# Hybrid attention and MoE layer: expert rows summed in four PSUM banks over the whole pass, picks that carry the row scale, more of expert 13 kept, half loads in the last turn

## The chip, the core and the metric

The kernel runs on one core of a Trainium2 chip. A core has TensorE (PE, matrix products into PSUM), VectorE (DVE), ScalarE (ACT), GpSimd (POOL) and SyncE (SP, which here only issues transfers), an on-chip memory SBUF of 128 partitions, and the accumulator memory PSUM with 8 banks of 128 x 512 floats. Transfers from HBM are issued on queues and carried by 16 DMA engines. The metric is the device time of one execution in microseconds; lower is better. The span of a profiled execution goes from its first to its last instruction.

## What is computed

One layer over 256 tokens plus 16 meta tokens, width 1024, in float32. First a mixer (two attentions side by side, gates, an output projection that is added to the residual), then a mixture of experts, and a final norm:

```python
h = h + mix[:, :T]
hn = rms_norm(h, norm_ffn_g[l])
# moe_ffn(hn): top 4 of 32 experts for each token, softmax over the four
gu = xb @ w_gate_up[e] + b_gate_up[e]                 # 1024 -> 2048
x_glu = minimum(x_glu, 7.0); x_lin = clip(x_lin, -7.0, 7.0)
act = x_glu * sigmoid(1.702 * x_glu) * (x_lin + 1)
yb = act @ w_down[e] + b_down[e]                      # 1024 -> 1024
out[token] += yb * gate
h = h + out
return rms_norm(h, norm_final_g)[:, N_META:]
```

Every expert is read whole: 8 MiB of gate-up weights and 4 MiB of down weights, 32 times, 403 MB in all.

## The kernel before, in words

**Stages.** Up to about 240 us the mixer runs; its weights come in through a ring of small slots. Then the residual `h1` (two tiles of 128 tokens) is normed, the router picks experts, and one pass over the 32 experts follows, until about 1152 us. Each expert has up to `CAP` = 64 rows in a pass; with more, a further pass would run (`n_pass`, read from memory at run time; here it is 1). Then come the final norm and four stores.

**Slots and loads.** The expert weights go through four slots of 4 MiB (`eslot(0)` to `eslot(3)`, two in the tensor `arena`, two in `ring`). A pass has 96 loads of one slot each, in the order gate-up first half, gate-up second half of an expert, and its down rows behind those of the next expert. SP waits until a slot is free (`slot_free`, on `wide_used`, which TensorE raises), then issues the load of four places later. The first eight refills are cut into quarters (`first_refill`), then come whole loads (`whole_load`), and `last_loads` cuts the last five into halves, the very last into a half and two quarters. TensorE waits for loads in `arrived`. `KEPT` = 3 of the eight gate-up chunks of expert 29 (3 MiB) are loaded ahead, during the mixer's end, into memory that is free by then, and left out of the load of that expert.

**The order on TensorE.** It is written out by hand. Ahead of the loop: projection, router products, counting of ranks in bank 7, and `gather_first`, which collects the rows of experts 0 and 1. A gather is a product of the row-scaled residual `hs` (made by ScalarE, in two copies) with a 0/1 matrix `pick` made by VectorE. Then `gate_up` of expert 0, a transposition of the biases and `features` (eight transpositions of rows into features). The loop goes over turns of two pairs of experts; `expert_pair` does, for experts x and x+1: `gate_up` of x+1, `pick_rows`, `down` of x, `gather` for the next pair, `scatter` of x, `gate_up` of x+2, `features`, `pick_rows`, `down` of x+1, `features`, `scatter`. `last_pair` is its end form. `scatter` multiplies the expert's rows with the gated pick and leaves the 256 x 1024 result in banks 4 to 7, and VectorE adds those banks to `h1` each time (`add_rows`, two additions of 128x1024 for an expert). TensorE waits for the first of them (`s_acc`) before it uses banks 4 to 7 again. After `BIAS_TURN` = 3 turns the gated down biases are multiplied once and added in the same way.

**The other engines.** VectorE also makes the picks, adds biases, clamps and forms the activation; ScalarE copies PSUM rows to SBUF and does the sigmoid. At the end VectorE multiplies `h1` by the final gain, which a transfer has put on all 128 partitions (`gfin`).

## Time and profile before

| what | us |
|---|---|
| median of 3 runs | 1165.92 (1164.47 to 4083.46) |
| the profiled execution, time | 1165.41 |
| its span | 1163.6 |
| TensorE busy | 1101.5 (95%) |
| VectorE, ScalarE busy | 332.2 (29%), 203.7 (18%) |
| read from HBM | 432.13 MB |

How to read it: TensorE's share is high, but its rows can overlap and waits between them are short, so the share alone doesn't say that it is the bound. The transfer rate in each slice of the span is the second thing to look at. A row of a timeline gives its start in us from the start of the span, its duration, the engine, the line of the program, the operation and how many instructions stand in it; in brackets is how long the engine was idle before it and what ended that. A matrix product of the source is two such instructions where its operands are full float32.

### The profile page before, as it was taken

The numbers are of one execution on the slowest core, as the hardware profiler recorded it, in microseconds if no ns is written. First come the engines' busy times: TensorE is split into PE (matmuls) and PEld (weight loads), VectorE is DVE, ScalarE is ACT, GpSimd is POOL, SyncE is SP. The second block draws the span as 40 slices with busy tenths as digits, with TensorE's granted clock in tenths as the row PEclk, the third lists the DMA queues.
The fourth block names the chain that finished last, engine by engine and source line by source line (L and its number), as shares of the span: only waits on it lengthen the run. The fifth ranks groups of instructions, "written<-read, shape, count | busy, mean of one in ns | idle before, by whom it ended". The sixth has DMA issues, their size and how long they took to land. (4 is left out here: it accounts for less than half of the span.)

```text
span 1163.6 us, 13610 instructions
## 1 busy us (share of the span) xinstructions
PE 1101.5 (95%) x5490; PEld 526.2 (45%) x5490; DVE 332.2 (29%) x774; ACT 203.7 (18%) x359; POOL 14.2 (1%) x27
## 2 busy tenths in 40 slices
PE   8999999999999989898989998989999999899997
PEld 6878888554343434343434343433333333343433
DVE  2256443132323131313131313131313131313223
ACT  2438781031101010101010101010101010101012
POOL 3010000000000000000000000000000000000000
PEclk9999999999999999999989999999999999999999
DMA  9814237869999999999999999999999999999994
GB/s 309 278 36 128 90 110 291 359 223 423 422 433 431 431 433 430 431 433 430 433 431 432 431 432 430 433 431 431 433 430 433 430 431 433 431 431 431 426 426 164
DMA packets 39750, 433.66 MB, mean 373 GB/s; under 512 B 3160, under 2 KB 19698, under 8 KB 23204
## 3 DMA queue, kind: packets, MB, share of 16 engines
q1 hardware_dynamic: 38160, 429.45, 88.1%
q0 software_dynamic: 960, 2.30, 0.6%
q10 hardware_dynamic: 596, 1.45, 0.4%
q8 instruction: 23, 0.38, 0.1%
q14 instruction: 11, 0.09, 0.0%
HBM read 432.13 MB, written 1.05 MB: 372 GB/s over the span
## 5 line engine op out<-in xcount | busy, mean ns | idle before, releaser
L1738 PE MATMUL psum<-arena 128*64 128x512 f32 x1016 | 224.4, 595 | 11.0 <-DMA arena<-in_w_gate_up 10.9
L1738 PE MATMUL psum<-ring,arena 128*64 128x512 f32 x968 | 217.4, 604 | 9.2 <-DMA ring<-in_w_gate_up 9.2
L1738 PEld LDWEIGHTS psum<-arena 128*64 128x64 f32 x1016 | 70.9, 137 | 156.8 <-issue 139.9
L1754 PE MATMUL psum<-ring,arena 128*64 128x512 f32 x544 | 123.7, 608 | 15.5 <-DMA ring<-in_w_down 9.1
L1738 PEld LDWEIGHTS psum<-ring,arena 128*64 128x64 f32 x968 | 68.2, 139 | 151.1 <-issue 148.8
L1196 DVE TENSOR_TENSOR arena<-psum,biasT 128x512 f32<-128x512 f32 x64 | 44.3, 692 | 292.3 <-PE psum L1710 288.0
L859 DVE TENSOR_TENSOR arena<-psum,vT 128x512 f32<-128x512 f32 (+1 forms) x42 | 28.4, 681 | 341.7 <-PE psum L1637 331.8
L1754 PE MATMUL psum<-arena 128*64 128x512 f32 x480 | 108.0, 603 | 10.4 <-DMA arena<-in_w_down 10.4
L773 ACT ACTIVATE arena<-psum 128x1024 f32<-128x1024 f32 x32 | 32.7, 1023 | 325.1 <-PE psum L1738 311.7
L1754 PEld LDWEIGHTS psum<-ring,arena 128*64 128x64 f32 x544 | 42.2, 140 | 85.5 <-issue 85.5
L1220 DVE TENSOR_TENSOR h<-h,psum 128x1024 f32<-128x1024 f32 x64 | 75.3, 1218 | 16.0 <-PE psum L1779 14.0
L1754 PEld LDWEIGHTS psum<-arena 128*64 128x64 f32 x480 | 35.0, 139 | 73.3 <-issue 67.6
L780 ACT ACTIVATE arena<-arena 128x512 f32<-128x512 f32 x32 | 20.2, 630 | 266.1 <-DVE arena L1204 266.1
L1779 PE MATMUL psum<-kst,wr 64*128 64x512 f32 x256 | 63.6, 615 | 1.6 <-ACT kst L790 1.6
L1637 PEld LDWEIGHTS psum<-arena 128*128 128x128 f32 x512 | 58.4, 192 | 12.9 <-issue 12.9
L1637 PE MATMUL psum<-arena 128*128 128x128 f32 x512 | 61.4, 279 | 0.0
L1587 PE MATMUL psum<-arena,ring 128*128 128x256 f32 x256 | 60.5, 380 | 0.0
L790 ACT ACTIVATE kst<-psum 128x512 f32<-128x512 f32 x32 | 19.1, 597 | 225.7 <-PE psum L1754 225.7
L1587 PEld LDWEIGHTS psum<-arena,ring 128*128 128x128 f32 x256 | 46.3, 190 | 5.6
L1710 PEld LDWEIGHTS psum<-kst,arena 128*128 128x128 f32 x256 | 27.4, 141 | 25.4 <-issue 24.3
L1710 PE MATMUL psum<-kst,arena 128*128 128x128 f32 x256 | 35.0, 280 | 0.8 <-ACT arena L773 0.8
L1779 PEld LDWEIGHTS psum<-kst,wr 64*128 64x128 f32 x256 | 22.2, 186 | 22.5 <-issue 20.7
(233 smaller groups left out, 762.2 us busy)
## 6 DMA issues: line engine op xcount, KB each, us to landing
arena<-in_w_gate_up SPq DMA_DIRECT2D x28, 4096.0 KB, 30.2
ring<-in_w_gate_up SPq DMA_DIRECT2D x27, 4096.0 KB, 30.0
arena<-in_w_down SPq DMA_DIRECT2D x14, 4096.0 KB, 30.1
ring<-in_w_down SPq DMA_DIRECT2D x12, 4096.0 KB, 30.1
ring<-in_w_in SPq DMA_DIRECT2D x14, 1024.0 KB, 12.5
arena<-in_w_gate_up SPq DMA_DIRECT2D x13, 1024.0 KB, 15.9
arena<-in_w_gate_up SPq DMA_DIRECT2D x5, 2048.0 KB, 25.2
ring<-in_w_down SPq DMA_DIRECT2D x10, 1024.0 KB, 16.4
```

The costliest lines, as they stand in the source:

```text
L773: sc.activation(gl.rearrange("q (b j p) -> q b j p", p=P, j=DN_ROWS), banks(home, home + 2).rearrange("q (b p j) -> q b j p", p=P, j=DN_ROWS),
L780: sc.activation(sg, glu, ACT.Sigmoid, scale=1.702).then_inc(s_sig, 1)
L790: sc.activation(yr, bank[1], ACT.Copy).then_inc(s_y, 1)
L859: return v.tensor_tensor(dst, src, vec.unsqueeze(2).broadcast_to([P] + cols), ALU.mult)
L1196: return v.tensor_tensor(dst.rearrange("p (m j) -> p m j", m=8), src, bias[:, m:m + 8, cols(e, 1)].broadcast_to([P, 8, CAP]), ALU.add)
L1220: v.tensor_tensor(half, half, banks(4 + 2 * t, 6 + 2 * t), ALU.add).then_inc(s_acc[t], 1)
L1587: ins = mm(job_bank(name)[:, 0:SEQ], win(8 + m // 2)[:, c, (m % 2) * P:(m % 2 + 1) * P], xnT[:, c, META:KEYS], start=c == 0, stop=c == CH - 1)
L1637: ins = mm(bank[k][:, c * P:(c + 1) * P], hs[:, t, (4 * k + c) * P:(4 * k + c + 1) * P], pick[:, t, :], start=t == 0, stop=t == 1)
L1710: ins = tr(bank[home + m // 4][:, (m % 4) * P:(m % 4 + 1) * P], gl[:, m * P:(m + 1) * P], ident)
L1738: ins = mm(bank[home + n][h * CAP:(h + 1) * CAP, :], xg[:, c, e * CAP:(e + 1) * CAP], w[:, h * D + n * 512:h * D + (n + 1) * 512], start=c ...
L1754: ins = mm(bank[1][n * CAP:(n + 1) * CAP, :], act[:, c * CAP:(c + 1) * CAP], w[:, n * 512:(n + 1) * 512], start=first, stop=last)
L1779: ins = mm(bank[4 + 2 * t + n], pickgT[n * CAP:(n + 1) * CAP, t * P:(t + 1) * P], yr[n * CAP:(n + 1) * CAP, :], start=True, stop=True)
```

## The change

- **Sums in PSUM.** Banks 4 to 7 hold the sum over all experts. Four products with a zero operand (`open_sum`) open them ahead of the loop, every `scatter` accumulates (`start=False`), the down biases accumulate too, and VectorE adds the banks to `h1` once, after the last expert, into `fin`. `add_rows` and its waits are gone. Behind the last gathers of a pass TensorE puts `fin - h1` back into the four banks for a further pass.
- **Other banks.** What used banks 4 to 7 moves: ranks to bank 3, the first `gate_up` and `features` to banks 2 and 3, the odd expert's `features` to banks 0 and 1, `pick_rows` to bank 0. New waits follow: `s_low` for the first expert, `s_pgt` before a gather, `s_lin` before the second `pick_rows`.
- **Picks carry the scale.** `hs` and ScalarE's two copies are gone. The pick matrices are multiplied by the row's scale, the gates are divided by it, and a gather reads `h1` itself, each fourth float (`strided`).
- **Kept rows.** The kept part is now of expert 13 (3 MiB of gate-up) and, new, three of its eight down chunks (1.5 MiB). The two loads that are shortened lie in turn 3, which is written out beside the loop.
- **The end.** The last ten loads, all of the last turn, are halves. The final gain is loaded to one partition and spread by two products in `last_pair`. `BIAS_TURN` is 4.

```diff
-KEPT_EXPERT = EXPERTS - 3
+KEPT_TURN = 3
+KEPT_EXPERT = 2 * UNROLL * KEPT_TURN + 1
+HALVES = TURN_LOADS - GU_LOADS
+KEPT_DN = 3
+KEPT_DN_LOAD = KEPT_LOAD + EXPERT_LOADS + 1
-BIAS_TURN = 3
+BIAS_TURN = KEPT_TURN + 1
...
-                    if idx == KEPT_LOAD:
-                        part_of(idx, rows, 0, QUARTERS - KEPT, whole)
-                    elif left > ESLOT:
+                    if left >= HALVES:
                         part_of(idx, rows, 0, QUARTERS, whole)
                     else:
                         part_of(idx, rows, 0, 2, half_loaded[left])
...
+                loops_of_loads(b, base, 0, kept_at)
+                for idx in range(REFILL_END + kept_at * TURN_LOADS, REFILL_END + (kept_at + 1) * TURN_LOADS):
+                    if idx not in (KEPT_LOAD, KEPT_DN_LOAD):
+                        whole_load(idx, base, 1)
+                        continue
+                    slot_free(idx, base)
+                    part = slice(0, EWIDTH - (KEPT * 2 * D if idx == KEPT_LOAD else KEPT_DN * D))
+                    sp.dma_start(eslot(idx)[:, part], rows_of(idx - GU_LOADS, 1)[:, part]).then_inc(
+                        wide_loaded[idx % ESLOT], 16)
+                loops_of_loads(b, base, kept_at + 1, LOAD_TURNS)
...
+            kept_down = down_rows(KEPT_EXPERT)
+            sp.dma_start(kept_dn[0], kept_down[:, EWIDTH - 3 * D:EWIDTH - 2 * D]).then_inc(s_kdn, 16)
+            sp.dma_start(arena[:, 0:2 * D], kept_down[:, EWIDTH - 2 * D:EWIDTH]).then_inc(s_kdn, 16)
...
-                sc.activation(hs[:, t, :].rearrange("q (b j p) -> q b j p", p=P, j=GU_ROWS),
-                              h1[:, t * D:(t + 1) * D].rearrange("q (b p j) -> q b j p", p=P, j=GU_ROWS),
-                              ACT.Copy, scale=st[:, 22 + t:23 + t]).then_inc(s_hs, 1)
...
+            def first_pick(t):
+                for e in range(2):
+                    ins = v.tensor_scalar(pick[:, t, e * CAP:(e + 1) * CAP], iota, rk3[:, t, e:e + 1],
+                                          st[:, 22 + t:23 + t], ALU.is_equal, ALU.mult)
+                return ins
...
+                for t in range(2):
+                    ins = v.tensor_scalar(pick[:, t, :], pick[:, t, :], st[:, 22 + t:23 + t], None, ALU.mult)
...
-            def add_rows(x):
-                for t in range(2):
-                    dve.wait_ge(s_sc, x * 2 + (t + 1))
-                    half = h1[:, t * D:(t + 1) * D]
-                    v.tensor_tensor(half, half, banks(4 + 2 * t, 6 + 2 * t), ALU.add).then_inc(s_acc[t], 1)
...
-                clamped(mlink, x, 0, 4)
+                clamped(mlink, x, 0, 2, s_low, dve.snap(b * PAIRS + 1))
...
+                v.tensor_copy(gains, banks(2, 4)).then_inc(s_gs, 1)
+                for t in range(2):
+                    dve.wait_ge(s_sc[t], x + EXPERTS)
+                    v.tensor_tensor(fin[:, t, :], h1[:, t * D:(t + 1) * D], banks(4 + 2 * t, 6 + 2 * t),
+                                    ALU.add).then_inc(s_acc[t], 1)
...
-                        ins = mm(bank[k][:, c * P:(c + 1) * P], hs[:, t, (4 * k + c) * P:(4 * k + c + 1) * P],
-                                 pick[:, t, :], start=t == 0, stop=t == 1)
+                        ins = mm(bank[k][:, c * P:(c + 1) * P],
+                                 strided(h1[:, t * D:(t + 1) * D], 4 * k + c, GU_ROWS), pick[:, t, :],
+                                 start=t == 0, stop=t == 1)
...
+            def open_sum(n):
+                mm(bank[n], fmask[:, 0:P], kst[:, 0:512], start=True, stop=False)
...
-                                 yr[n * CAP:(n + 1) * CAP, :], start=True, stop=True)
-                    ins.then_inc(s_sc, 1)
+                                 yr[n * CAP:(n + 1) * CAP, :], start=False, stop=last)
+                    ins.then_inc(s_sc[t], 1)
...
-                for t in range(2):
-                    pe.wait_ge(s_acc[t], x + 1)
+                pe.wait_ge(s_lin, g + 1)
                 pick_rows(x + 1, 1)
-                down(tb, o + 5, x + 1, half_loaded[ESLOT] if ending else None)
+                down(tb, o + 5, x + 1, ending, part_kept)
...
+                for n in range(2):
+                    ins = mm(bank[2 + n], ones[96:97, :], gfin[:, n * 512:(n + 1) * 512], start=True, stop=True)
+                ins.then_inc(s_gb, 1)
                 scatter(x)
...
+                pe.wait_ge(s_minus, 1)
+                for t in range(2):
+                    pe.wait_ge(s_acc[t], b + 1)
+                    for n in range(2):
+                        col = slice(n * 512, (n + 1) * 512)
+                        mm(bank[4 + 2 * t + n], ident, fin[:, t, col], start=True, stop=False)
+                        ins = mm(bank[4 + 2 * t + n], minus, h1[:, t * D + n * 512:t * D + (n + 1) * 512], start=False,
+                                 stop=False)
+                ins.then_inc(s_again, 1)
```

Three places show how instructions move. First TensorE, ahead of the loop over the passes, from the rank count of the second tile's first half to the first `gate_up`. Before (1645 is `gather_first`, 1628 the router, 1695 and 1696 the rank count):

```order
L1645 MATMUL psum<-arena 128x128 x4
L1628 MATMUL psum<-wr,arena 128x32 x4
L1645 MATMUL psum<-arena 128x128 x4
L1695 MATMUL psum<-rk,kst 128x32
L1696 MATMUL psum<-rk,kst 128x32
L1645 MATMUL psum<-arena 128x128 x4
L1701 TENSOR_LOAD npi
L1701 ISA x2
L1645 MATMUL psum<-arena 128x128 x4
```

And now (1675 is `gather_first`, 1657 the router, 1728 `open_sum`, 1733 and 1734 the rank count):

```order
L1675 MATMUL psum<-arena,h 128x128 x4
L1657 MATMUL psum<-wr,arena 128x32 x4
L1675 MATMUL psum<-arena,h 128x128 x4
L1728 MATMUL psum<-kst 128x512
L1733 MATMUL psum<-rk,kst 128x32
L1734 MATMUL psum<-rk,kst 128x32
L1728 MATMUL psum<-kst 128x512 x2
L1675 MATMUL psum<-arena,h 128x128 x4
L1728 MATMUL psum<-kst 128x512
L1742 TENSOR_LOAD npi
L1742 ISA x2
L1675 MATMUL psum<-arena,h 128x128 x4
```

Four openings stand between the rank count and the last gather, and the gathers read `h`. Second, SP's queue between the mixer's last weights and the first refills, now (590 and 597 are expert 0's and 1's gate-up loads, 592 and 599 kept gate-up rows, 594 and 595 are new):

```order
L590 DMA arena<-in_w_gate_up 128x8192 x2
L592 DMA arena<-in_w_gate_up 128x2048
L594 DMA arena<-in_w_down 128x1024
L595 DMA arena<-in_w_down 128x2048
L597 DMA ring<-in_w_gate_up 128x8192
L599 DMA arena<-in_w_gate_up 128x4096
L585 DMA ring<-in_w_gate_up 128x4096
```

The two new loads stand behind the first kept one and ahead of a wait. Third, the end of TensorE's program. Before (1754 is `down`, 1779 `scatter`, 1748 `pick_rows`, 1637 `gather`):

```order
L1754 MATMUL psum<-ring,arena 64x512 x16
L1779 MATMUL psum<-kst,wr 128x512 x4
L1748 MATMUL psum<-kst,arena 128x128 x2
L1754 MATMUL psum<-ring,arena 64x512 x16
L1779 MATMUL psum<-kst,wr 128x512 x4
L1637 MATMUL psum<-arena 128x128 x16
```

And now (1802, 1832, 1796 and 1666 in their places; 1906 spreads the gain, 1927 and 1928 put the sums back):

```order
L1802 MATMUL psum<-ring,arena 64x512 x16
L1906 MATMUL psum<-arena,kst 128x512 x2
L1832 MATMUL psum<-kst,wr 128x512 x4
L1796 MATMUL psum<-kst,arena 128x128 x2
L1802 MATMUL psum<-ring,arena 64x512 x16
L1832 MATMUL psum<-kst,wr 128x512 x4
L1666 MATMUL psum<-arena,h 128x128 x16
L1927 MATMUL psum<-arena,kst 128x512
L1928 MATMUL psum<-h,vraw 128x512
L1927 MATMUL psum<-arena,kst 128x512
```

Two products come between the down rows of expert 30 and their `scatter`, and eight (the pair of rows four times) behind the last gathers.

## Rows read from the trace of the kernel before

**Rows 1.** The page: span, busy times, and GB/s in 40 slices.

```profile
span 1163.6 us, 13610 instructions
PE 1101.5 (95%) x5490; PEld 526.2 (45%) x5490; DVE 332.2 (29%) x774; ACT 203.7 (18%) x359; POOL 14.2 (1%) x27
GB/s 309 278 36 128 90 110 291 359 223 423 422 433 431 431 433 430 431 433 430 433 431 432 431 432 430 433 431 431 433 430 433 430 431 433 431 431 431 426 426 164
```

**Rows 2.** Stretches: length, busy PE, PEld, DVE, ACT, POOL, clock, DMA share, GB/s.

```profile
360.00:600.00 240.00, 221.28 (x1092) 88.64 (x1092) 59.69 (x101) 22.99 (x37) 0.00 (x0) 1.00 1.00 432
...
1096.00:1106.00 10.00, 10.00 (x52) 3.77 (x50) 3.44 (x6) 0.63 (x1) 0.00 (x0) 1.00 1.01 429
```

**Rows 3.** Timelines of TensorE and SP's queue, and one piece of the chain.

```profile
617.94 0.33 SPq L507 DMA_DIRECT2D ring<-in_w_gate_up  x1
...
663.01 13.96 PE L1738 MATMUL psum<-arena 128*64 128x512 f32 x64
...
684.29 3.84 PE L1637 MATMUL psum<-arena 128*128 128x128 f32 x32
...
715.36 7.09 PE L1738 MATMUL psum<-ring,arena 128*64 128x512 f32 x32
...
705.28 30.02 DMA arena<-in_w_down
```

**Rows 4.** Timeline of the routing, and one stretch of it (columns as in rows 2).

```profile
185.41 0.43 SPq L567 DMA_DIRECT2D arena<-in_w_gate_up  x1
...
230.00:240.00 10.00, 9.76 (x42) 5.61 (x40) 4.68 (x15) 3.50 (x4) 0.00 (x0) 1.00 0.02 10
...
239.63 0.33 SPq L561 DMA_DIRECT2D ring<-in_w_gate_up  x1
243.11 2.13 ACT L752 ACTIVATE arena<-h,st 128x1024 f32<-128x1024 f32 x1 [0.23 <-DVE st L1100]
...
245.16 0.41 PE L1695 MATMUL psum<-rk,kst 128*128 128x32 f32 x2 [0.41 <-DVE rk L1114]
246.48 1.16 PE L1645 MATMUL psum<-arena 128*128 128x128 f32 x8 [0.69 <-DVE arena L1061]
248.00 1.15 PE L1645 MATMUL psum<-arena 128*128 128x128 f32 x8 [0.36 <-issue]
249.16 13.10 PE L1738 MATMUL psum<-arena 128*64 128x512 f32 x60
251.14 5.48 SPq L490 DMA_DIRECT2D arena<-in_w_down  x4
```

**Rows 5.** Groups by form and a timeline row, 227 to 252 us.

```profile
228.07 3.60 PE L1606 MATMUL psum<-ring,arena 128*128 128x512 f32 x8
...
L1645 PEld LDWEIGHTS psum<-arena 128*128 128x128 f32 x32 | 3.9, 192 | 1.3 <-DVE arena L1061 0.8 <-issue 0.6
L1618 PEld LDWEIGHTS psum<-kst,h 128*128 128x128 f32 x16 | 2.5, 215 | 0.9 <-issue 0.9
```

**Rows 6.** The end: the last load waited for, and TensorE.

```profile
1024.19 31.69 DMA arena<-in_w_down
1056.01 7.09 PE L1754 MATMUL psum<-arena 128*64 128x512 f32 x32 [0.95 <-DMA arena<-in_w_down]
...
1144.00:1148.00 4.00, 4.00 (x20) 1.40 (x20) 1.81 (x2) 0.39 (x1) 0.00 (x0) 1.00 0.08 35
...
1144.57 7.09 PE L1754 MATMUL psum<-ring,arena 128*64 128x512 f32 x32
1154.37 3.84 PE L1637 MATMUL psum<-arena 128*128 128x128 f32 x32
```

**Rows 7.** The bias step and VectorE's additions.

```profile
602.01 6.58 PE L1892 MATMUL psum<-arena,kst 32*128 32x512 f32 x8 [2.81 <-DVE h L1220]
600.00:610.00 10.00, 7.99 (x12) 2.70 (x14) 5.62 (x7) 0.00 (x0) 0.00 (x0) 0.63 1.01 434
L1220 DVE TENSOR_TENSOR h<-h,psum 128x1024 f32<-128x1024 f32 x64 | 75.3, 1218 | 16.0 <-PE psum L1779 14.0
```

More of the change, by code:

```diff
@@ L363, in build @@
         s_y = sem("down_rows_in_sbuf")
-        s_sc = sem("rows_scattered")
+        s_sc = [sem(f"rows_of_tile{t}_scattered") for t in range(2)]
         s_acc = [sem(f"rows_of_tile{t}_added") for t in range(2)]
@@ L531, in last_loads, with loops_of_loads @@
                             part_of(idx, rows, 3, QUARTERS, whole)
+            def loops_of_loads(b, base, first, last):
+                with sp.Fori(first, last) as j:
+                    turn = j * (QUARTERS * TURN_USES) + base
+                    if not isinstance(b, int):
+                        turn = sp.snap(turn)
+                    for o in range(TURN_LOADS):
+                        whole_load(REFILL_END + o, turn, j * (2 * UNROLL) + 1)
             def whole_pass(b):
@@ L1257, in _ @@
                         expert_pair(mlink, tb, u, j, False)
-                for t in range(2):
-                    dve.wait_ge(s_bm, b * 2 + (t + 1))
-                    half = h1[:, t * D:(t + 1) * D]
-                    v.tensor_tensor(half, half, banks(4 + 2 * t, 6 + 2 * t), ALU.add).then_inc(s_ba[t], 1)
-                for t in range(2):
-                    dve.wait_ge(s_ba[t], b + 1)
                 v.memset(st[:, 50:51], 0.0)
@@ L1725, in gate_up @@
                         pe.wait_ge(s_xg, fresh + (c // 4 + 1))
-                    if j == 0:
+                    if c == 4 and between is not None:
+                        between()
+                    if ending and j == 0:
+                        first_half(o + k)
+                    if j == (GU_ROWS // 2 if ending else 0):
                         arrived(tb, o + k)
@@ L1756, in down_chunk, with down, scatter @@
                 return ins
[L1758 removed]
+            def down(tb, o, x, ending=False, part_kept=False):
                 pe.wait_ge(s_act, x + 1)
[L1761 removed]
+                if ending:
+                    first_half(o)
+                else:
                     arrived(tb, o)
[L1763 to L1764 removed]
                 idx = GU_LOADS + o
                 for c in range(CH):
[L1767 removed]
+                    if ending and c == CH // 2:
                         arrived(tb, o)
[L1769 removed]
+                    w = eslot(idx)[:, c * D:(c + 1) * D]
+                    if part_kept and c >= CH - KEPT_DN:
+                        if c == CH - KEPT_DN:
+                            pe.wait_ge(s_kdn, 32)
+                        w = kept_dn[c - (CH - KEPT_DN)]
+                    ins = down_chunk(c, w, c == 0, c == CH - 1)
                     if c % 2 == 1:
                         used(ins, idx)
[L1773 removed]
+            def scatter(x, last=False):
                 pe.wait_ge(s_pgt, x + 1)
@@ L1882, in _ @@
                 parts[0] = None
+                tb = pe.snap(b * TURNS + KEPT_TURN)
+                for u in range(UNROLL):
+                    expert_pair(tb, u, False, u == 0)
                 for t in range(2):
@@ L1886, in _ @@
                 pe.wait_ge(s_bdn, 16)
-                for t in range(2):
-                    pe.wait_ge(s_acc[t], x + 4 * BIAS_TURN)
                 pe.wait_ge(s_gT, b + 1)
```

164 lines of the change are left out of this document (83 added, 81 removed).

## The prediction

> **What bounds the kernel now.** I first read the page: the span is 1163.6 us, TensorE is busy for 95% of it, and from the tenth slice on the core reads 422 to 433 GB/s in every slice but the last [rows 1]. Two resources are nearly full, so the question is which one ends last. The stretches answer it: 432 GB/s from 360 to 600 us and 429 GB/s around 1100 us, with a DMA share of 1.00 and 1.01 [rows 2]. TensorE has gaps in the first of them (221 us busy of 240). A pair of experts needs 52.35 us of TensorE where nothing is waited for (the same place of the loop starts at 663.01 and 715.36 [rows 3]). It needs 24 MiB = 25.2 MB, which is 58.3 us at 432 GB/s. So the weight stream is the bound by 5.9 us a pair. One stream of expert weights starts with the first released quarter at 251.14 us [rows 4] and runs without a break to about 1146 us (35 GB/s are left from 1144 to 1148 [rows 6]). The end is then: where the stream starts, plus its bytes, plus what TensorE and the output still do after it. A queue of transfers also covers TensorE's lateness: a load of 4 MiB takes 9.7 us of the stream (4.19 MB / 432), but landed 30.02 us after its issue at 705.28 us [rows 3], so it waited behind two others.
>
> **The start of the stream.** The first quarter is released by the first pick-weighted products of expert 0, which begin at 249.16 us [rows 4]. Ahead of them the change puts four opening matmuls of 128x128 by 512. The trace has this form in the output projection: 8 instructions in 3.60 us, 0.43 us apart [rows 5]. A source-level matmul of this form is two instructions (the four chunks of a first gather are 8), so one opening costs 0.86 us and four 3.43 us. TensorE idles here for 0.41, 0.69 and 0.36 us, 1.46 us in all [rows 4], and the openings can fill these. That leaves 2.0 us. If the sequencer's gaps are counted from issue to issue they are 0.5, 0.8 and 0.55 us, and 1.6 us are left.
>
> The residual is now read as the stationary operand with a stride of four floats. The trace has that read too: its weight loads take 215 ns, against 192 ns for the packed ones of the gather [rows 5]. I take it that a gather runs at the pace of its weight loads (32 instructions in 3.84 us [rows 3]), so that each instruction comes 0.023 us later: 0.2 us for 8, 0.4 us for the two first gathers on the path, 0.75 us for the 32 of a pair. The dropped scaled copies gain nothing: the second ended at 243.11 + 2.13 = 245.2 us, and the gather that used it started at 246.48 us, released by the pick [rows 4]. The extra small operations of VectorE lie beside the openings. So the stream starts **2.1 us later**, with 0.5 (openings nearly all in gaps) and 3.8 us (nothing covered) as bounds.
>
> Here a rule of the Trainium skill speaks against the change. "SBUF — State Buffer", on SBUF cachelines, says that a line holds 16 bytes, that full bandwidth needs at least two hits in one, and that each access that crosses to a new line pays a penalty; a stride of four floats crosses at every element. The page gives the penalty no size. By that rule, the trace agrees in sign with its 215 against 192 ns [rows 5], and by the row the sum gets the 0.4 and 0.75 us above; the rule in its full form would be the rival (c) below.
>
> The new wait of TensorE for expert 0's features (banks 2 and 3 are reused at once) holds back expert 1 by two bias additions and some small operations, about 2.1 us. By then 8 MiB are queued since 253 us, which last until some 273 us, and the next release, the first quarter of expert 1 at about 267.5 us before, would be at 267.5 + 2.1 + 2.1 = 271.7 us. It is hidden, with little to spare; if the cover failed it would cost at most 2 us.
>
> **The extra 1.5 MiB kept.** They are asked for right behind the first kept rows, at 186 us. From 230 to 240 us the transfers carry 10 GB/s, 0.1 MB in all, so they are done at about 230.2 us; the next load is issued at 239.63 us [rows 4]. 1.57 MB at 430 GB/s move the end to 233.9 us, into the gap. So nothing is late, and the main stream has 1.57 MB less: **3.65 us less** at 432 GB/s.
>
> Moving the kept part from expert 29 to expert 13 takes 4.5 MiB = 4.72 MB, 10.9 us, out of the stream at once, in the middle. That is harmless only if a slot is always free. Counting back from the landing at 735.30 us with 9.7 us a load, the load issued at 617.94 us landed at about 638 us, 20 us after issue [rows 3]: the shortest wait I find, and just after the bias step, where TensorE was idle for 2.81 us, then ran its bias matmuls in 6.58 us and had a clock of 0.63 from 600 to 610 us [rows 7]. Now that step stands a turn later and waits for no VectorE addition; four matmuls need 3.4 us. I followed the slots through the turn of expert 13, with TensorE's times of [rows 3] and 9.7 us for 4 MiB: the tightest load has its slot freed at about 635 us and is reached by the stream at about 648 us, so 10 us of queue are left and no idle time appears.
>
> Between the experts TensorE no longer waits for additions, but nothing is gained there: it waits for loads anyway. The VectorE additions dropped (64 of 1218 ns, 75 us [rows 7]) are off the path but for the last. 0.75 us more per gather lie in the 5.9 us a pair of slack.
>
> **The end.** Before, the down rows of expert 27 arrive at 1055.88 us (issue 1024.19 plus 31.69), and from 1056.01 TensorE never waits for data again; its last down rows are done at 1144.57 + 7.09 = 1151.7 us [rows 6]. After: 1055.9 + 2.1 - 10.9 = 1047.1 us. Ten loads follow, 40 MiB = 41.9 MB, 98.2 us at the 427 GB/s or so of this end (426 in two slices, 429 in the stretch [rows 1, 2]), so the last lands at 1145.3 us. TensorE alone would need 95.7 us and be done before that, so the stream sets the end. The half loads let it follow closely. The second half of expert 31's gate-up lands 19.5 us before the last byte. Then 3.5 us of chunks, 2.1 us to the down chunks (row copy and transposes), 7.0 of them, 1.7 for broadcasting the gain in two new matmuls (it covers the 0.75 us wait for the copy of the down rows), 1.9 for the sum, 0.4 for picks, 7.0 for the last down. Together 23.6 us, and 24.3 with a wait of 0.7 for the second half of expert 30's down rows: 4.8 us after the last landing, at 1150.1 us. That is **1.6 us earlier** than before (3.65 less for bytes, 2.1 more for the start, and nothing to speak of from the halves).
>
> After it, before: the last sum, the spare gathers from 1154.37 to 1158.21 us [rows 6], beside them VectorE's two additions, the norm and the stores, with which the span ends at 1163.6 us [rows 1]. After, the output chain is some 0.4 us shorter (rank update and gain moved ahead). But TensorE gets eight more matmuls of 128x128 by 512 behind its gathers, which put the sums back into PSUM for a next pass that does not come: 16 instructions of 0.43 us = 6.9 us. It would end at 1158.2 + 0.75 + 6.9 = 1165.8 us on the old time axis, past the 1163.6 us of the output. So the tail becomes **2.2 us longer**, and TensorE, not the store, ends the span.
>
> **The sum**, against the profiled execution's 1165.41 us (its span and 1.8 us around it; the median shown, 1165.92 us, is 0.5 us above): + 2.1 - 3.65 + 2.2 = +0.65, so **1166.0 us**.
>
> **Rivals.** (a) The tail's matmuls don't set the end, or the openings fall into gaps. Then the output chain ends last, 1150.1 + 11.9 - 0.4 = 1161.6 us span, 1163.4 us of time; with a start only 0.5 us late, 1161.8 us. For it: the restore matmuls produce nothing that is read. Against: they stand ahead of TensorE's end of program. (b) The change doesn't shorten the stream: at expert 13 the queue runs dry, because a slot is released late, or a clock drop as at 600 us [rows 7] makes TensorE late at its new first wait for expert 0's features. The whole 3.65 us are then lost: 1169.7 us. Against: 10 us of queue. (c) Strided weight loads are slow when each is one of many. Beyond 5.9 us more per gather TensorE is the bound; if each took four times 192 ns, a gather would grow from 3.8 to 24.6 us and each of 15 pairs by 20.8 - 5.9 = 14.9 us: 1166 + 223 = 1389 us. The rows speak against it, with 23 ns instead of 576 [rows 5]. It is what the cacheline rule of the Trainium skill's page "SBUF — State Buffer" would mean if each element cost a whole line. (d) Faster by over 2% needs 23 us; only a stream faster than 432 GB/s gives that, and no row shows one.
>
> **Chances.** The forecast 0.58, (a) 0.25, (b) 0.12, (c) 0.04, (d) 0.01. The stream's rate has its own spread: 0.3% of 890 us is 2.7 us. The range goes from (a) to (b): 1161.3 to 1170. A measurement of this kernel tells 2% from no change, 23 us; so faster 0.01, same 0.95, slower 0.04.
>
> **What would show it.** Expert 0's first product at 251 us instead of 249.2; no slice from 260 to 1140 us under 420 GB/s, above all around expert 13 (about 600 to 640 us); last landing at 1144 to 1146 us; gather groups of 4.2 to 4.6 us; TensorE's 16 last instructions after the output chain, ending the span. Wrong would be: gathers over 9.7 us, DMA gaps in the turn of expert 13, or an output store that ends last.

## The result, and the profile after

| | time, median us | ratio to before, 95% interval | span of the profiled execution |
|---|---|---|---|
| before | 1165.76 | | 1163.6 |
| after | 1179.55 (1176.24 to 1179.64) | 1.0117 [1.0105, 1.0129] | 1174.4 |

The kernel is slower by 1.2%, which is 13.6 us above the 1166.0 us predicted and outside the range of 1161.3 to 1170. (The 4083.46 us among the times of before is a single outlier, which the median leaves out.) The profiled execution of after is the fastest of its runs, 1176.24 us; what is known of the 3.3 us more of the others is told under "The openings".

From the page of after: its busy times, its rates in 40 slices, the make-up of the chain that ended last, its costliest weight loads, and one row of its issues:

```profile
PE 1165.7 (99%) x5518; PEld 590.1 (50%) x5518; DVE 266.6 (23%) x747; ACT 199.5 (17%) x357; POOL 14.3 (1%) x27
GB/s 306 280 32 143 73 109 323 375 180 422 405 427 413 434 431 430 431 435 434 429 430 428 426 431 429 427 419 430 433 432 430 435 431 430 434 426 427 427 425 95
PE 92%; DMA 5%; DVE 2%; issue 0%; ACT 0%; SPq 0%; DVEq 0%; ACTq 0%
L1666 PEld LDWEIGHTS psum<-arena,h 128*128 128x128 f32 x512 | 120.7, 329 | 12.9 <-issue 12.9
arena<-in_w_gate_up SPq DMA_DIRECT2D x27, 4096.0 KB, 20.1
```

The same chain in the page of before, the row of the gathers' weight loads and the row of issues:

```profile
PE 29%; DMA 18%; ACT 0%; issue 0%; DVE 0%; SPq 0%; ACTq 0%; DVEq 0%
L1637 PEld LDWEIGHTS psum<-arena 128*128 128x128 f32 x512 | 58.4, 192 | 12.9 <-issue 12.9
arena<-in_w_gate_up SPq DMA_DIRECT2D x28, 4096.0 KB, 30.2
```

Read the weight loads first: the same 512 loads of the gathers took 192 ns each and now take 329. Then the chain: DMA falls from 18% to 5% of the span and TensorE has 92%. (The shares of before add up to 47% only, so the chain found there covers less than half of the span; the waits below are the stronger evidence.) The bound has changed sides. The rates look as before [rows 1], so a reader who looks at bandwidth alone sees nothing: 430 GB/s in the middle. But each load of 4 MiB now lands 20.1 us after its issue, not 30.2, because one load less waits ahead of it: SP gets its slots late. Stretches of after against [rows 2]:

```profile
360.00:600.00 240.00, 240.00 (x1114) 103.08 (x1112) 43.61 (x94) 20.84 (x33) 0.00 (x0) 1.00 1.00 430
```

TensorE's 18.7 us of idle time in this stretch are gone, and the granted clock is 1.00, as before, so the slower weight loads are not a slower clock. Over the whole pass, before first and then after:

```profile
252.00:1144.00 892.00, 841.50 (x4100) 330.91 (x4096) 225.60 (x383) 82.10 (x129) 0.00 (x0) 0.99 1.00 429
```

```profile
252.00:1144.00 892.00, 888.16 (x4105) 384.00 (x4106) 159.98 (x357) 81.51 (x128) 0.00 (x0) 1.00 1.00 425
```

Before, TensorE had 50.5 us of idle time in 892 us; after, 3.8 us are left. The waits of TensorE tell the same. Before, the largest of four rows of waits for expert loads, which hold 39.6 us together (columns: the line that waits and what it waits for, total us, times, longest):

```profile
PE psum L1738 <- DMA arena<-in_w_gate_up: 10.9, 5, 2.3
```

After, the largest wait of the pass and its only one for a load of an expert:

```profile
PE psum L1788 <- DVE arena L1239: 2.0, 1, 2.0
...
PE psum L1802 <- DMA ring<-in_w_down: 0.2, 1, 0.2
```

The timeline of TensorE after, around the start of the pass, at one pair of experts, and at the end:

```profile
244.11 2.11 PE L1675 MATMUL psum<-arena,h 128*128 128x128 f32 x8
...
247.28 1.96 PE L1728 MATMUL psum<-kst 128*128 128x512 f32 x4
249.07 1.90 PE L1675 MATMUL psum<-arena,h 128*128 128x128 f32 x8
...
251.68 1.90 PE L1675 MATMUL psum<-arena,h 128*128 128x128 f32 x8
...
407.19 7.73 PE L1666 MATMUL psum<-arena,h 128*128 128x128 f32 x32
...
1149.69 7.09 PE L1802 MATMUL psum<-ring,arena 128*64 128x512 f32 x32
1157.57 1.99 PE L1832 MATMUL psum<-kst,wr 64*128 64x512 f32 x8 [0.79 <-ACT kst L816]
1159.49 7.73 PE L1666 MATMUL psum<-arena,h 128*128 128x128 f32 x32
1167.06 1.02 PE L1927 MATMUL psum<-arena,kst 128*128 128x512 f32 x2
...
1173.07 1.02 PE L1928 MATMUL psum<-h,vraw 128*128 128x512 f32 x2
```

Expert 0's `gate_up` starts at 253.51 us, 4.35 us later than before [rows 4]. A gather of 32 instructions takes 7.73 us, not 3.84 [rows 3]. The last down rows end at 1149.69 + 7.09 = 1156.8 us, 5.1 us later than before [rows 6], and from there to the end of the span it takes 17.6 us instead of 11.9. So the 10.8 us of span are 5.1 us up to the last product of weights and 5.7 us of tail.

The 5.1 us can be split once more. `gate_up` of expert 1 starts at 271.99 us in after (the row stands under "The openings") and started here before:

```profile
265.53 13.96 PE L1738 MATMUL psum<-ring,arena 128*64 128x512 f32 x64
```

That is 6.5 us later. From there to the end of the last down rows after takes 884.8 us and before took 886.1. The slower gathers, 58 us more of them, thus filled what TensorE had left unused in the pass; what they cost is that nothing is left to hide the later start, the 3.65 us of saved stream gain nothing, and the last gathers are slow too.

### The profile page after: what moved, and what is told of

Same layout as the page of the kernel before. It is cut to its first block, busy times and chain, and to the rows that moved or that the text cites. A ratio compares the mean times of both kernels' runs of the same rounds, so it can differ in the third digit from the quotient of the medians.

```text
span 1174.4 us, 13519 instructions
## 1 busy us (share of the span) xinstructions
PE 1165.7 (99%) x5518; PEld 590.1 (50%) x5518; DVE 266.6 (23%) x747; ACT 199.5 (17%) x357; POOL 14.3 (1%) x27
## 3 DMA queue, kind: packets, MB, share of 16 engines
HBM read 431.61 MB, written 1.05 MB: 368 GB/s over the span
## 4 chain that ended last, share of the span: by engine, by line
PE 92%; DMA 5%; DVE 2%; issue 0%; ACT 0%; SPq 0%; DVEq 0%; ACTq 0%
PE psum L1788 36%; PE psum L1802 18%; PE psum L1666 10%; PE psum L1832 5%; DMA ring<-in_w_down 5%; PE psum L1616 4%; PE psum L1416 2%; PE psum L1751 2%; PE psum L1595 2%; PE psum L1635 2%; PE psum L1374 1%; PE psum L1578 1%; PE psum L1796 1%; PE psum L1675 1%; DVE arena L1024 1%; DMA h<-in_x 1%
## 5 line engine op out<-in xcount | busy, mean ns | idle before, releaser
L1788 PE MATMUL psum<-ring,arena 128*64 128x512 f32 x968 | 214.2, 598 | 2.0 <-DVE arena L1239 2.0
L1788 PEld LDWEIGHTS psum<-ring,arena 128*64 128x64 f32 x968 | 67.9, 138 | 140.3 <-issue 139.6
L1666 PEld LDWEIGHTS psum<-arena,h 128*128 128x128 f32 x512 | 120.7, 329 | 12.9 <-issue 12.9
L1666 PE MATMUL psum<-arena,h 128*128 128x128 f32 x512 | 123.7, 400 | 0.0
L1802 PE MATMUL psum<-ring,arena 128*64 128x512 f32 x532 | 118.1, 595 | 0.3 <-DMA ring<-in_w_down 0.2
L1802 PEld LDWEIGHTS psum<-ring,arena 128*64 128x64 f32 x532 | 37.1, 137 | 69.3 <-issue 68.4
L1416 PE MATMUL psum<-arena,ring 128*128 128x272 f32 (+1 forms) x128 | 29.0, 387 | 0.0
## 6 DMA issues: line engine op xcount, KB each, us to landing
arena<-in_w_gate_up SPq DMA_DIRECT2D x27, 4096.0 KB, 20.1
```

Source lines behind the costliest of these rows:

```text
L1416: ins = mm(job_bank(name)[:, 0:width], win(s)[:, c, k * P:(k + 1) * P], xnT[:, c, cols:cols + width], start=c == 0, stop=c == CH - 1)
L1666: ins = mm(bank[k][:, c * P:(c + 1) * P], strided(h1[:, t * D:(t + 1) * D], 4 * k + c, GU_ROWS), pick[:, t, :], start=t == 0, stop=t == 1)
L1788: ins = mm(bank[home + n][h * CAP:(h + 1) * CAP, :], xg[:, c, e * CAP:(e + 1) * CAP], w[:, h * D + n * 512:h * D + (n + 1) * 512], start=c ...
L1802: ins = mm(bank[1][n * CAP:(n + 1) * CAP, :], act[:, c * CAP:(c + 1) * CAP], w[:, n * 512:(n + 1) * 512], start=first, stop=last)
```

## The experiments

Two theories were set against each other. **A**: the strided weight loads of the gathers make TensorE the bound. **B**: the gathers are harmless, and the openings, the new waits and the late start of the stream cost the time. Below, "after" is the changed kernel, ratios are to the kernel before on the same chip (medians 1164.9 to 1165.8 us), and each kernel has its name in brackets.

### Is the stream still the bound?

```diff
-KEPT_DN = 3
+KEPT_DN = 1
...
```

(e0_kept1) The kept down rows shrink from 1.5 to 0.5 MiB, so 1 MiB more goes through the stream; this also frees the memory that the next experiment needs.

> The changed kernel with one kept down chunk of expert 13 (0.5 MiB) instead of three: 1 MiB more in the stream, 2.4 us at 432 GB/s. Theory A (TensorE is the bound of the changed kernel, because a strided gather takes 7.73 us instead of 3.84): the stream has room, so the time stays at 1176 to 1180 us, moved by under 1 us. Theory B (the stream still sets the end, and what was lost lies in its late start and in the opening products): it ends 2.4 us later, 1179 to 1182 us.

Measured: 1179.19 us, 1.0119 [1.0102, 1.0136], against 1179.55 us for after. The number lies in the ranges of both theories (B's begins at 1179), so it is the difference that tells: 1.05 MB are 2.4 us of stream at 430 GB/s, and the median moved by -0.4 us. TensorE waits for no load of an expert in the trace. The stream doesn't bind in after, but it is close behind: the fastest run of this kernel took 1177.46 us, 1.2 us more than the fastest of after, both with a mean granted clock of 0.999. With one such run each this may be chance or the first sign of the other bound.

### The stride alone, taken away and put in

(e1_packed) From the previous kernel, a packed copy of the residual (unscaled) is made by ScalarE again and the gathers read it (TensorE waits for each copy before its first gathers; these lines are left out here):

```diff
+                sc.activation(hs[:, t, :].rearrange("q (b j p) -> q b j p", p=P, j=GU_ROWS),
+                              h1[:, t * D:(t + 1) * D].rearrange("q (b p j) -> q b j p", p=P, j=GU_ROWS),
+                              ACT.Copy).then_inc(s_hs, 1)
...
-                                 strided(h1[:, t * D:(t + 1) * D], 4 * k + c, GU_ROWS), pick[:, t, :],
+                                 hs[:, t, (4 * k + c) * P:(4 * k + c + 1) * P], pick[:, t, :],
```

> As e0_kept1, but ScalarE makes a packed, unscaled copy of the residual again and the gathers read it (it needs the 1 MiB that e0_kept1 gives up). Theory A: gathers of 3.8 us, weight loads of 192 ns, TensorE waits for loads again; start of the stream 2 us after that of the kernel before, and the restoring products in the tail still cost 2 us: 1164 to 1168 us, 10 us or more below e0_kept1. Theory B (openings, new waits and late start cost the time, the stride little): within 4 us of e0_kept1.

Measured: 1166.78 us, 1.0016 [1.0007, 1.0026]. The packed reads take back 12.4 of the 14.1 us that e0_kept1 lay above before. The page's chain and the largest of its waits, the first `gate_up` and a gather of the loop:

```profile
PE 70%; DMA 26%; DVE 2%; issue 1%; ACT 0%; SPq 0%; DVEq 0%; ACTq 0%
...
PE psum L1808 <- DMA ring<-in_w_down: 11.5, 9, 2.4
...
250.58 13.95 PE L1794 MATMUL psum<-arena 128*64 128x512 f32 x64
...
293.10 3.84 PE L1670 MATMUL psum<-arena 128*128 128x128 f32 x32
```

DMA is back in the chain, the waits for loads are back, and loads land 28.6 to 30.1 us after issue. The other way round (e6_before_strided), one thing changed in the kernel before: ScalarE leaves the scaled copy in natural order and the gathers read each fourth float of it.

```diff
-                sc.activation(hs[:, t, :].rearrange("q (b j p) -> q b j p", p=P, j=GU_ROWS),
-                              h1[:, t * D:(t + 1) * D].rearrange("q (b p j) -> q b j p", p=P, j=GU_ROWS),
-                              ACT.Copy, scale=st[:, 22 + t:23 + t]).then_inc(s_hs, 1)
+                sc.activation(hs[:, t, :], h1[:, t * D:(t + 1) * D], ACT.Copy,
+                              scale=st[:, 22 + t:23 + t]).then_inc(s_hs, 1)
...
-                        ins = mm(bank[k][:, c * P:(c + 1) * P], hs[:, t, (4 * k + c) * P:(4 * k + c + 1) * P],
+                        ins = mm(bank[k][:, c * P:(c + 1) * P], strided(hs[:, t, :], 4 * k + c, GU_ROWS),
```

> The kernel before with one thing changed: ScalarE's scaled copy is left in its natural order, and the gathers read it with the stride of four floats. Theory A: each gather takes 7.7 us instead of 3.84; 15 of them are 58 us of TensorE, of which its waits for loads (40 us in all) and its slow-clock stretches behind them take up most: about 10 to 14 us more, 1175 to 1179 us, TensorE never waiting for a load, issue to landing near 20 us. Theory B (the stride alone is harmless, it needed the new openings and waits): under 4 us more, 1165 to 1169 us.

Measured: 1174.42 us, 1.0078 [1.0063, 1.0094]. This edit alone costs 9.4 us, just under the 10 us that A's interval began with and far from B's. Its waits, a gather of the loop, and the last two first-gathers in one row:

```profile
PE psum L1890 <- DVE h L1218: 2.8, 1, 2.8
PE psum L1752 <- DMA ring<-in_w_down: 2.1, 1, 2.1
...
246.36 4.10 PE L1643 MATMUL psum<-arena 128*128 128x128 f32 x16 [0.69 <-DVE arena L1059]
...
289.23 7.73 PE L1635 MATMUL psum<-arena 128*128 128x128 f32 x32
```

3.5 us of waits for loads are left of some 40 (2.1 and, in a row not shown, 1.4). The gather takes 7.73 us although it reads the scaled copy in `arena` and not `h1`, so it is the stride and not the tensor. The first row shows a side of the change that I had priced at nothing: once TensorE is the bound, its waits for VectorE cost their full length. In this kernel the bias step is 2.81 us of idle time, 7.19 us of products and a `gate_up` of 16.77 us behind them; in the profiled execution of after the same three are 0.72, 3.69 and 13.95. That is 8.4 us between these two executions. Only 2.1 us of it are the shorter wait; 6.3 us are the lower granted clock behind it (0.50 from 610 to 620 us in this kernel, with nothing of the kind in the trace of after). The shorter wait is the gain of the sums in PSUM that is shown. The clock part is not: of the eight other traces with the sums in PSUM and the same 0.72 us wait, one lost nothing to the clock at this step and seven lost 1.65 to 3.4 us. Before itself lost 5.1 us there, hidden by its waits for loads.

### What a stride costs

(e7_strides) Behind the last gathers of after stand eight spare products for each of five strides. Their results are not used; the span is longer by them. The kernel was run once, in 1192.13 us, 15.9 us more than the fastest run of after; the spare products take 14.7 us of it.

```diff
+                def column(s):
+                    return h1[:, 0:P * s].rearrange("q (p j) -> q j p", j=s)[:, 0, :]
+                for _ in range(8):
+                    mm(bank[0][:, 0:P], column(1), pick[:, 0, :], start=True, stop=True)
...
+                for _ in range(8):
+                    mm(bank[0][:, 0:P], column(16), pick[:, 0, :], start=True, stop=True)
```

> The changed kernel with spare products behind the last gathers, 8 for each stride of 1, 2, 4, 8 and 16 floats in the stationary operand (their results are not used). If the cost comes with the 16-byte line as the Trainium skill's page on SBUF has it: weight loads of 192 ns at strides 1 and 2 (two hits a line), 329 ns at 4 and the same at 8 and 16. If it grows with the distance: rising from 2 to 16. Time as of the changed kernel plus up to 15 us for the spare products.

Measured, by line and form (busy us, mean ns of one); 1925, 1927, 1929, 1931 and 1933 have strides of 1, 2, 4, 8 and 16 floats:

```profile
L1931 PEld LDWEIGHTS psum<-arena,h 128*128 128x128 f32 x16 | 3.9, 337 | 0.0
L1929 PEld LDWEIGHTS psum<-arena,h 128*128 128x128 f32 x16 | 3.8, 328 | 0.0
L1933 PEld LDWEIGHTS psum<-arena,h 128*128 128x128 f32 x16 | 3.6, 312 | 0.0
L1927 PEld LDWEIGHTS psum<-arena,h 128*128 128x128 f32 x16 | 2.0, 196 | 0.0
L1925 PEld LDWEIGHTS psum<-arena,h 128*128 128x128 f32 x16 | 1.9, 193 | 0.0
...
1170.10 2.05 PE L1927 MATMUL psum<-arena,h 128*128 128x128 f32 x16
1171.99 3.90 PE L1929 MATMUL psum<-arena,h 128*128 128x128 f32 x16
```

It is a step, not a slope: strides 1 and 2 are alike, then the load takes 1.7 times as long, and a longer stride adds nothing (16 is a little quicker). The products behind the loads come 0.12 us apart at strides 1 and 2 and 0.23 us at 4 (1.89 and 3.73 us for 16, from start to start): the load grew by 132 ns and the pace by some 115 ns, so nearly all of the longer load passes into the pace. The granted clock was 1.00 in all five groups, and the packed one reads `h1` too. So neither the clock nor the tensor makes the difference. The Trainium skill's "SBUF — State Buffer", on SBUF cachelines, has lines of 16 bytes and asks for two hits in each; four-byte floats at a stride of two give two hits and at four give one. By that rule the step lies between 2 and 4, and the trace agrees, with 196 and 328 ns.

### The openings

(e4_openlater) The four `open_sum` products move from ahead of the stream's start to behind expert 0's `features`, for the first pass only:

```diff
-            wait_emptied(pe, last_jobs[4])
-            open_sum(4)
...
                 features(x, 2)
+                with pe.If(b < 1):
+                    for n in range(4, 8):
+                        open_sum(n)
```

> The changed kernel; the four opening products stand behind the features of expert 0, where TensorE waits 2.04 us for VectorE, instead of ahead of the first gate-up products. Theory A (TensorE is the bound from there on): their 3.4 us fill the wait, the clock does not fall there, and all of TensorE's chain moves by 2.0 us for the wait and 1.4 us for the clock: 3 to 4 us less. Theory B (the stream sets the end): the stream starts 3 us earlier, 3 us less too, but then TensorE waits for loads again. The chain of waits tells them apart.

Measured: 1176.24 us, 1.0097 [1.008, 1.0114], 3.3 us less than after. Around the start of the pass:

```profile
247.30 4.00 PE L1675 MATMUL psum<-arena,h 128*128 128x128 f32 x16 [0.93 <-DVE arena L1094]
251.23 13.95 PE L1782 MATMUL psum<-arena 128*64 128x512 f32 x64
...
267.50 3.60 PE L1728 MATMUL psum<-kst 128*128 128x512 f32 x8
271.03 13.95 PE L1782 MATMUL psum<-ring,arena 128*64 128x512 f32 x64
...
PE psum L1796 <- DMA ring<-in_w_down: 1.4, 1, 1.4
```

`gate_up` of expert 0 starts 2.3 us earlier, and the openings fill the time in which after waits 2.04 us for VectorE. In after, the first products of expert 1 then ran slower (15.38 us); in this kernel they did not (13.95 us), and they are done 2.4 us earlier. Both theories forecast 3 us less; the waits decide for A, with a single one of 1.4 us for a load. Such a fall of the granted clock shows in these kernels now and then behind a short idle time. In after, beside the wait of 2.04 us:

```profile
271.99 15.38 PE L1788 MATMUL psum<-ring,arena 128*64 128x512 f32 x64 [2.04 <-DVE arena L1239]
...
724.51 3.69 PE L1956 MATMUL psum<-arena,kst 32*128 32x512 f32 x8 [0.72 <-ACT kst L846]
728.13 13.95 PE L1788 MATMUL psum<-ring,arena 128*64 128x512 f32 x64
```

and the bias step in this kernel (the first two rows) and in e0_kept1, there with a mean granted clock of 0.83 of the upper level (2.4 GHz) in that stretch:

```profile
722.13 3.90 PE L1953 MATMUL psum<-arena,kst 32*128 32x512 f32 x8 [0.72 <-ACT kst L846]
725.96 15.39 PE L1782 MATMUL psum<-ring,arena 128*64 128x512 f32 x64
...
724.93 5.25 PE L1955 MATMUL psum<-arena,kst 32*128 32x512 f32 x8 [0.72 <-ACT kst L845]
730.11 15.75 PE L1787 MATMUL psum<-ring,arena 128*64 128x512 f32 x64
...
720.00:740.00 20.00, 19.28 (x70) 6.61 (x68) 5.23 (x15) 1.49 (x3) 0.00 (x0) 0.83 0.99 427
```

The same code and the same 0.72 us wait took 1.56 + 1.80 = 3.4 us more in e0_kept1 than in the profiled execution of after, and 1.65 us more in this kernel. With TensorE as the bound that goes into the time, and 3.4 us is the size of what parts the fastest run of after, 1176.24 us, from its median, 1179.55. That the other runs of after had this fall is inferred; they have no trace, but their mean granted clock was 0.996 and that of the fastest 0.999, and of e0_kept1's four runs the one with 0.999 was the fastest too.

So the 3.3 us between the medians are not the openings' alone. The profiled executions of the two kernels took the same time, 1176.33 us here and 1176.24 in after: this one was 2.4 us ahead behind expert 1's `gate_up`, lost 1.65 us at the bias step, and 1.2 us more at its wait for a load. The 2.4 us are what the trace shows for moving the openings; how much of them reaches the end depends on the clock at the bias step and on a stream that is close behind.

### The tail

(e2_norestore) After, with the restore products under the condition of a second pass; as `n_pass` is 1 they are skipped, and nothing of the output depends on them.

```diff
+                with pe.If(n_pass > 1):
+                    pe.wait_ge(s_minus, 1)
+                    for t in range(2):
...
-                ins.then_inc(s_again, 1)
+                    ins.then_inc(s_again, 1)
```

> The changed kernel; the eight products behind the last gathers that put the sums back into PSUM run only if a further pass follows (it does not). If TensorE's tail sets the end: the last gathers end at about 1167.1 us on the changed kernel's axis and the last store at about 1169 us, so 5 us less, 1171 to 1174.5 us. If the tail is not on the path: no change.

Measured: 1174.23 us, 1.0086 [1.0069, 1.0103], 5.3 us less than after (its four runs spread from 1171.95 to 1176.22). The products take 6.9 us. Before, the spare gathers ended at 1158.2 us, 5.4 us ahead of the end of the span; the slow gathers use up 3.9 of these, 1.5 are left, and 6.9 - 1.5 = 5.4 us show, close to the 5.3 measured. The trace agrees: from the end of the last down rows to the end of the span it is 11.9 us again, as before, and was 17.6 in after.

### What is left without openings and tail

With both the late openings and the whole tail (gathers too) skipped in a single pass, once with the strided and once with packed reads (the latter with 0.5 MiB of kept down rows). First strided (e9_strided_rest):

> The changed kernel with both other mends (openings later, tail only for a further pass), the strided gathers kept. What is left above the kernel before is then the stride's: if TensorE sets the end, 1168 to 1172 us; if the stride were harmless, 1161 to 1163 us.

Measured: 1169.78 us, 1.0043 [1.0027, 1.0058]; a single wait for a load in the pass, of 0.2 us. So the stride's price is not one number: 12.4 us with openings and tail as in after, 9.4 us in the kernel before, and here some 4.4 us against the packed kernel that follows. Then packed (e5_best):

> e1_packed with the openings behind expert 0's features, and the last gathers and restoring products only if a further pass follows. The stream sets the end: it starts as in the kernel before, carries 1 MiB less for that of e0_kept1's kept part (0.5 MiB against the kernel before, 1.2 us), and the output chain is 0.4 us shorter: 1162 to 1164.5 us, 1 to 3 us below the kernel before. Theory B as for e1_packed: no better than 1174.

Measured over 11 runs: 1165.4 us, 1.0000 [0.9991, 1.0009]. I had expected 1 to 3 us under before, and missed. Its start shows one reason. With the openings gone from there, TensorE stands idle again, and its next gather runs at a lower clock (2.07 us for what took 1.15 before; granted clock 0.87 from 247 to 249 us and 0.50 from 249 to 251, against 1.00 before):

```profile
247.35 1.16 PE L1679 MATMUL psum<-arena 128*128 128x128 f32 x8 [0.93 <-DVE arena L1098]
248.87 2.07 PE L1679 MATMUL psum<-arena 128*128 128x128 f32 x8 [0.36 <-issue]
...
253.33 5.48 SPq L505 DMA_DIRECT2D arena<-in_w_down  x4
```

The stream's first quarter is issued at 253.33 us, against 251.14 us before and 252.56 us in e1_packed, where the openings stand ahead. The start was to be that of before, so 2.2 us of the miss are here; that is more than the 1.2 us of kept rows could pay for. So the last one (e10_packed_notail) puts the openings back there and keeps packed reads and the skipped tail:

```diff
-                pe.wait_ge(s_pick, g + 1)
-                gather(0)
-                gather(1)
+                with pe.If(n_pass > 1):
+                    pe.wait_ge(s_pick, g + 1)
+                    gather(0)
+                    gather(1)
...
```

> e1_packed, and its last gathers and restore products stand under the condition of a second pass, so that in this one-pass execution the program skips them; the openings stay ahead of the stream. Theory A (the stride was the main cost; with packed reads the rest is the tail): in e1 the last product started at 1165.64 and ended the span, while the last store was issued at 1161.48 us; without the products the output chain ends last, some 2 us after that issue, so the span falls by 2 to 3.5 us: 1163.3 to 1165.3 us in time, against 1166.8 for e1 and 1165.0 for the kernel before. Theory B (the run's end is set by how far the stream was behind, whatever TensorE does after its last scatter): within 0.5 us of e1, 1166.3 to 1167.3 us. Beside it the same kernel with later openings gave 1165.4; if the openings ahead of the stream cost with packed reads what they cost with strided ones (3.3 us), this one comes at 1168 or more; if they are hidden by the queue of loads, at or under 1165.4.

Measured over 11 runs: 1165.52 us, 1.0002 [0.9993, 1.0011]; 1.3 us less than with the tail. That is 0.2 us above A's range and 0.8 us below B's, so it speaks for A without hitting it; the intervals of e1_packed and of this kernel just overlap. Openings ahead of the stream or behind it now give the same (1165.52 and 1165.4 us). With packed reads and without the tail, the rest of the change is thus worth nothing that can be measured here, in either direction, with 0.5 MiB kept extra; the tail costs about 1.3 us there. 1.5 MiB do not fit beside the packed copy, and a version with both was not built. None beats the kernel before.

## Why the prediction was wrong, point by point

**The step that failed** is "its weight loads take 215 ns, against 192 ns for the packed ones of the gather [rows 5]". The 215 ns are of L1618, a transposition with a strided operand; the 192 ns are of L1645, an ordinary product with a packed one. Two things differed, the operation and the layout, and I read them as one. The trace of before had the like pair: a transposition with a packed operand.

```profile
L1710 PEld LDWEIGHTS psum<-kst,arena 128*128 128x128 f32 x256 | 27.4, 141 | 25.4 <-issue 24.3 <-ACT arena L773 1.0
```

141 against 215 ns is a factor of 1.5; on 192 ns it would have given some 293 ns, or 3.2 us more for 32 loads, most of the real loss. The term "0.75 us for the 32 of a pair" measured 7.73 - 3.84 = 3.89 us, or 0.122 us for each instruction where 0.023 was taken.

**The second step that failed** is the slack: "0.75 us more per gather lie in the 5.9 us a pair of slack". 3.89 us would seem to lie in it too. But 5.9 us is the difference of two ideal periods. Over the pass the idle time was 50.5 us, not 15 times 5.9 = 88 us. One reason is that the pass starts with its slots full: from 252 to 360 us TensorE had no idle time at all (108.00 us busy of 108.00). Another is that it did not run at full pace between its waits. From 360 to 600 us it idled 18.7 us, 4.5 us a pair, and behind a wait its work could take longer, as these down rows do, which take 7.09 us elsewhere (granted clock 0.50 from 852 to 854 us):

```profile
851.90 8.72 PE L1754 MATMUL psum<-arena 128*64 128x512 f32 x32 [2.18 <-DMA arena<-in_w_down]
```

Fifteen gathers in the loop add 15 x 3.89 = 58.4 us: more than 50.5. With the mis-sized term (15 x 0.75 = 11 us) the error did not matter; with the true one it decides. TensorE's own time from expert 1 on now makes the end: 271.99 us, 15 pairs of 56.26 us, 4.4 us for the bias step and 1.4 us for the clock fall lead to 1121.7 us, and `gate_up` of expert 31 starts at 1122.08.

**The start**: 2.1 us predicted, 4.35 measured. The openings went as told, in pieces of 0.86 us. The three last first-gathers take 1.90 to 2.11 us instead of some 1.15 each, 0.85 us more instead of 0.2, and TensorE's 1.46 us of waits filled up as predicted: 3.43 + 3 x 0.85 - 1.46 = 4.5 us. The openings' own part is right in sign and a little large: in e1_packed, with packed gathers, expert 0's `gate_up` starts at 250.58 us, 1.4 us later than before, where 2.0 was predicted. The wait for expert 0's features was predicted at 2.1 us and measured 2.04; it was "hidden" by a queue of loads only in a kernel bound by loads. Here it counts, with 1.43 us of lower clock behind it.

**Kept rows, expert 13, halves**: right. From 230 to 240 us the transfers now carry 51 GB/s, and the next load is issued at 239.39 us:

```profile
230.00:240.00 10.00, 9.76 (x44) 5.83 (x43) 4.67 (x15) 1.35 (x3) 0.00 (x0) 1.00 0.12 51
```

In the turn of expert 13, 600 to 720 us, after waits for no load. With packed reads the stream keeps its 425 to 437 GB/s there, and TensorE's only wait for a load is one of 2.26 us at 670 us, which is TensorE ahead of the stream and not a gap in the stream. The 3.65 us of saved stream are real but worth nothing while TensorE is the bound; the first experiment, with 1 MiB less kept, says the same. The last bytes landed at about 1150 us instead of at 1145.3 (25 GB/s are left from 1150 to 1152 us), since slots were freed late.

**The tail**: the mechanism was right and its size wrong. TensorE's restore products end the span, past the store issued at 1165.01 us. Predicted was 2.2 us more, measured 5.7: the last gather adds 3.9 instead of 0.75 us, which is 3.15 of the 3.5 us between them.

**Dropped additions**: "nothing is gained there" was right only for a kernel bound by the stream. In the strided case the wait at the bias step is 2.1 us shorter and counts in full. The other 6.3 us of the 8.4 above are clock and differ from execution to execution.

**Rivals**: (a) and (b) assume a stream-bound pass and fall. Of (b), the clock drop at the new first wait did come, 1.43 us in the trace, but it took time from TensorE and left no gap in the stream (DMA share 0.99 to 1.04 from 270 to 276 us). (c) had the mechanism, a gather so slow that TensorE is the bound, but I let it begin at 5.9 us per gather and priced it with loads of four times 192 ns. By the idle time of the pass it begins at 50.5 / 15 = 3.4 us, and less with a later start. Even the like pair of transpositions (3.2 us) would have put the pass at that limit, so a case "both bounds meet, a few us to 15 us slower" was missing between the forecast and (c), and was what happened. The range would not have held it either: its lower end, 1161.3 us, is 0.5 us under the lowest case worked out, and nothing stretched its upper end beyond (b).

## What to carry to other kernels

Compare a row with one that differs in a single thing (operation, type, layout), and where there is none, look for a pair of rows elsewhere that does. Take an engine's slack from its idle time over the whole loop, not from one period times the number of periods. When the second resource idles for only 6% of the loop, price each edit under both bounds: here the openings and the tail, worth nothing measurable and 1.3 us with packed gathers, were worth some 2.4 and 5.3 us with strided ones. And where two medians differ by 3 us, compare the granted clocks too before the edit gets the credit.

## What the runs showed of the hardware

- A 128x128 float32 weight load takes 193 ns packed, 196 ns at a stride of two floats, and 328, 337 and 312 ns at strides of 4, 8 and 16; the products behind it come 0.22 to 0.24 us apart instead of 0.12 (e7_strides). For a transposition it is 215 ns at a stride of four and 141 ns packed (before).
- The strided gather hardly feels the clock. In e6_before_strided 16 of its instructions took 4.10 us at a granted clock of 0.50 (247 to 251 us), and 16 at stride 4 took 3.90 us at 1.00 in e7_strides. Eight packed ones took 2.07 us at the low clock (e5_best) and 1.15 at the high one (before).
- A load's time from issue to landing fell from 30.2 to 20.1 us at an unchanged 430 GB/s: the rate does not tell which side is late, the queue does.
- After idle times of 0.4 to 2.8 us the granted clock fell in some executions and not in others of nearly the same kernel. Behind the same 0.72 us wait at the bias step nothing was lost in after and e7_strides, 1.65 to 1.7 us in e1_packed, e2_norestore, e4_openlater, e9_strided_rest and e10_packed_notail, and 3.4 us in e0_kept1 and e5_best. Behind 2.81 us it was 5.1 us in before and 6.3 in e6_before_strided.
